# Gate table of the experts: one full fp32 product per token replaced by two rounded ones, and the work between them spread differently

## The chip, the cores and the metric

One NeuronCore of one Trainium2 chip runs the whole program in one launch. The metric is the device time in microseconds (us), median of three runs. Engines are named as the profile names them: PE (TensorE) with its weight loads PEld, DVE (VectorE), ACT (ScalarE), POOL (GpSimd) and SP (the queue that issues most DMAs).

## What is computed

Two transformer blocks on 512 tokens of width 1024. The part that the change touches is the expert layer of the first block: each token picks 128 experts (8 heads, 16 each) out of 16,384 = 128 x 128, with a gate value for each.

```python
    gate = jax.nn.softmax(top_s, axis=-1)
    def expert_block(args):
        xb, eb, gb = args
        act = jax.nn.gelu(jnp.einsum("pd,ped->pe", xb, jnp.take(u, eb, axis=0)), approximate=False)
        return jnp.einsum("pe,ped->pd", (gb * act).astype(v.dtype), jnp.take(v, eb, axis=0))
```

The kernel computes it densely: all 16,384 products u·x, a dense table of gates (zero where an expert was not picked), the product of both, and the dense product with v.

## The kernel before

The expert phase is the function `peer`. Activations lie transposed, features on the 128 partitions and the 512 tokens along a row. It has three parts.

**Front.** PE works through 16 query tiles and 128 "up" tiles of expert rows u. A tile is 24 matmuls (128x128 weights, 512 columns): a full fp32 product is made of three products of rounded fp32 (`F32R`), high x high, high x low, low x high (`parts_product`, L1125). The tile's way is fixed by semaphores: SP loads it into one of four ring slots, ACT writes its rounded high part (`high`, L1579), POOL subtracts to get the low part (L1451, 128x1024), PE multiplies, ACT applies Gelu from PSUM (L1593), SP stores the result to DRAM. High and low parts are double buffered: the parts of tile n+2 are made after PE has finished tile n. DVE meanwhile finds the top 16 of each head. `U_HEAD` = 6 up tiles per head are used there, `AHEAD` = 5 more before the gate table starts.

**Gate table.** The picked experts lie in `sel` (row number, column number, gate value, each 128 picks x 512 tokens after the transposes at L1539, copied from PSUM into `selt` by L1720). For each token the 128x128 gate table is a matrix product over its 128 picks: `rows` (0/1, 128 picks x 128) as the one operand, `cols` (the gate value where the column number fits, else zero) as the other. Eight tokens form a group, 64 groups in all. For a group DVE writes `rows` with one instruction (L1726, 128x1024, into half of the tile `h`) and `cols` with eight (L1730, 128x128 each, compare and multiply with two values per partition), PE makes eight plain fp32 matmuls of 128 columns (L1518, `gate`), ACT copies the group out of PSUM into `slab` (L1602). `rows`, `cols` and PSUM are double buffered: DVE may write group g once PE has finished g-2; PE may write group g once ACT has stored g-2. After every 16 groups (128 tokens, one of four stretches `tt`) ACT issues four DMAs of 2 MB that store the slab to DRAM (L1630), and waits for them before it stores the first group of the next stretch.

PE's program interleaves gate groups and up tiles by hand: `between(g)` says after which groups an up tile follows, `TAILS` how many follow after the sixteenth group of a stretch. Before, `between` is true for g % 8 in (0, 1, 3, 4, 6) and `TAILS` is (8, 8, 8, 11). The same two tables order ACT's Gelu and `high` work.

**Down.** 128 tiles of v, multiplied with gate table times activation; it begins after the last up tile.

Of the kernel before, what the change touches and what calls it, by code (L numbers as in the profile page):

```python
# [9 lines left out]
F32R = mybir.dt.float32r  # L10
ALU = mybir.AluOpType
# [3 lines left out]
P = 128  # L15
T = 512
# [1304 lines left out]
def peer(nc, K, d, ring):  # L1321
# [12 lines left out]
    with Phase(nc, "peer") as ph:  # L1334
# [1 line left out]
        wp = ph.sb("w_parts", [P, 2, 2, KT * P], F32R)  # L1336
        pp = ph.sb("act_parts", [P, 2, 2, T], F32R)
        slab = ph.sb("slab", [P, NKEY, P])
        sel = ph.sb("sel", [P, 3, TT, P])
        selt = ph.sb("selt", [P, 3, T])  # L1340
        cols = ph.sb("cols", [P, 2, G, NKEY])
        iota = ph.sb("iota", [P, NKEY])
        keys = ph.sb("keys", [P, 2, NKEY])
        stage = K.h[:, 0:4, :]
        rows = K.h[:, 4:8, :].rearrange("p (b x) t -> p b (x t)", b=2).rearrange("p b (g i) -> p b g i", g=G)

        flat = slab[:].rearrange("p i t -> p (i t)")
        at = [0]
# [51 lines left out]

        EARLY = PEER_H * U_HEAD
        AHEAD = 5
        TAILS = (8, 8, 8, 11)

        def between(g):

            return g % 8 in (0, 1, 3, 4, 6)

        assert EARLY + AHEAD + sum(TAILS) + TT * sum(between(g) for g in range(groups)) == U_TILES

# [64 lines left out]
        def _(pe):  # L1475
# [35 lines left out]
            def gate(g):  # L1511
                b = g % 2
                pe.wait_ge(rows_done, g + 1)
                pe.wait_ge(cols_done, g + 1)
                if g >= 2:
                    pe.wait_ge(g_stored, g - 1)
                for t in range(G):
                    last = nc.tensor.matmul(g_ps[:, b * 1024 + t * P:b * 1024 + (t + 1) * P], rows[:, b, t, :], cols[:, b, t, :],  # L1518
                                            start=True, stop=True)
                last.then_inc(g_done, 1)  # L1520

            n = 0
# [139 lines left out]
        def _(dve):  # L1662
# [55 lines left out]
            for w in range(3):  # L1718
                dve.wait_ge(tr_done, w + 1)
                V.tensor_copy(selt[:, w, :], t_ps[:, w * T:(w + 1) * T]).then_inc(tr_stored, 1)  # L1720
            dve.wait_ge(tr_stored, 3)
            for g in range(TT * groups):
                b = g % 2
                if g >= 2:
                    dve.wait_ge(g_done, g - 1)
                V.tensor_tensor(rows[:, b], iota[:].unsqueeze(1).to_broadcast([P, G, NKEY]),  # L1726
                                selt[:, 0, g * G:(g + 1) * G].unsqueeze(2).to_broadcast([P, G, NKEY]), ALU.is_equal).then_inc(rows_done, 1)
                for t in range(G):
                    one = slice(g * G + t, g * G + t + 1)
                    last = V.tensor_scalar(cols[:, b, t, :], iota[:], selt[:, 1, one], selt[:, 2, one], ALU.is_equal, ALU.mult)  # L1730
                last.then_inc(cols_done, 1)

            def weigh(n):
# [1140 lines left out]
```

## Time and profile before

| | |
|---|---|
| median of 3 runs | 4344.9 us (4344.23 to 4344.94) |
| profiled execution | 4345.56 us, its span 4344.0 us |
| PE busy / DVE / ACT / POOL, share of span | 88% / 53% / 38% / 23% |
| stretch of the gate table, 1531.6 to 2055.6 us | 524.0 us, PE busy 523.98 |
| DVE busy there | 295.3 us |
| POOL busy there | 179.0 us |

The granted clock of TensorE is 1.00 (2.4 GHz) through the whole stretch. A row of the groups reads: line, engine, operation, written tile <- read tiles, sizes, count | busy time in us, mean ns of one | idle time of the engine before it and what ended it. Plain fp32 matmuls at L1518 leave two records each, so 512 products show as x1024. Matmuls overlap in the pipeline: the pace is the distance between starts, not the mean duration.

### The profile page before, as it was taken

The page shows a single profiled execution, that of the slowest core. Times are in us where ns is not written, and L with a number is a line of the kernel's source. Part 1 is how long each engine was busy: PE and PEld are TensorE (multiplying, and loading weights), DVE is VectorE, ACT ScalarE, POOL GpSimd, SP SyncE. Part 2 cuts the span into 40 slices and gives each one's busy share as a digit, 9 for nine tenths or more (in the row PEclk, how much of TensorE's full clock was granted, in tenths as well). Part 3 has the DMA queues.
Part 4 walks back from the last instruction along what each step waited for, and adds up shares of the span by engine and source line. Part 5 has one row for each costly group of instructions (what it writes and reads, how often), then busy time and mean ns, then how long its engine had stood idle before and what let it go on. Part 6 is the DMA issues. An engine that isn't in the chain of part 4 may idle for free. (4 is left out here: it accounts for less than half of the span.)

```text
span 4344.0 us, 48140 instructions
## 1 busy us (share of the span) xinstructions
PE 3825.2 (88%) x17810; PEld 3089.1 (71%) x17810; DVE 2296.6 (53%) x3538; ACT 1670.5 (38%) x2292; POOL 1011.1 (23%) x560
## 2 busy tenths in 40 slices
PE   2999799789899999999999999777799963688998
PEld 1888677677688888887888888445577743566775
DVE  6555344445466576553777777423434346835242
ACT  6555454443322254443444444323322132333222
POOL 0222121153244433333444444100000014200000
PEclk9999899899999999999999999889899986899999
DMA  4111011144244434556888888300122221122221
GB/s 147 59 50 53 27 54 39 54 169 159 81 129 129 133 133 162 191 194 221 262 268 264 266 265 266 112 26 23 63 87 82 78 68 27 30 68 77 87 86 60
DMA packets 225918, 515.93 MB, mean 119 GB/s; under 512 B 23200, under 2 KB 98208, under 8 KB 223552
## 3 DMA queue, kind: packets, MB, share of 16 engines
q1 hardware_dynamic: 202336, 407.83, 29.5%
q0 software_dynamic: 18864, 68.69, 4.8%
q10 hardware_dynamic: 4528, 36.89, 2.1%
q8 instruction: 117, 1.92, 0.2%
q14 instruction: 73, 0.60, 0.0%
HBM read 439.15 MB, written 69.21 MB: 117 GB/s over the span
## 5 line engine op out<-in xcount | busy, mean ns | idle before, releaser
L1125 PE MATMUL peer_banks<-peer_h_parts,peer_w_parts 128*128 128x512 f32 x3456 | 800.3, 391 | 18.0 <-POOL peer_w_parts L1451 18.0
L1125 PEld LDWEIGHTS peer_banks<-peer_h_parts,peer_w_parts 128*128 128x128 f32 x3456 | 646.3, 188 | 151.4 <-POOL peer_w_parts L1451 18.8
L1125 PE MATMUL peer_banks<-peer_act_parts,peer_w_parts 128*128 128x512 f32 x3072 | 699.1, 390 | 9.4 <-DVE peer_act_parts L1745 9.4
L1125 PEld LDWEIGHTS peer_banks<-peer_act_parts,peer_w_parts 128*128 128x128 f32 x3072 | 578.3, 188 | 130.2 <-issue 9.8
L1451 POOL TENSOR_TENSOR peer_w_parts<-peer_raw,peer_w_parts 128x1024 fp32r<-128x1024 f32 x144 | 345.2, 2397 | 573.6 <-ACT peer_w_parts L1579 573.6
L1579 ACT ACTIVATE peer_w_parts<-peer_raw 128x1024 fp32r<-128x1024 f32 x272 | 286.9, 1055 | 390.7 <-PE peer_banks L1125 390.7
L1125 PE MATMUL mlp_ps<-h_parts,mlp_w_parts 128*128 128x512 f32 x1536 | 369.8, 404 | 46.5 <-DVE h_parts L1272 37.3
L1125 PE MATMUL mlp_ps<-hidden,mlp_w_parts 128*128 128x512 f32 x1536 | 365.0, 400 | 23.2 <-DVE mlp_w_parts L1253 23.2
L1125 PEld LDWEIGHTS mlp_ps<-h_parts,mlp_w_parts 128*128 128x128 f32 x1536 | 296.1, 193 | 121.0 <-DVE mlp_w_parts L1253 49.0
L1125 PEld LDWEIGHTS mlp_ps<-hidden,mlp_w_parts 128*128 128x128 f32 x1536 | 292.5, 191 | 95.7 <-issue 25.0
L175 POOL TENSOR_TENSOR peer_slab<-peer_slab 128x1024 f32<-128x1024 f32 x96 | 236.8, 2467 | 335.9 <-ACT peer_slab L182 335.6
L1740 DVE TENSOR_TENSOR peer_slab<-peer_slab 128x512 f32<-128x512 f32 x128 | 294.9, 2304 | 4.4 <-DMA peer_slab<-peer_gates 4.4
L1125 PE MATMUL hgrn_proj_ps<-h_parts,hgrn_w_parts 128*128 128x512 f32 x960 | 269.0, 412 | 21.1 <-POOL hgrn_w_parts L469 21.1
L1750 DVE TENSOR_TENSOR peer_w_parts<-peer_raw,peer_w_parts 128x1024 fp32r<-128x1024 f32 x128 | 156.9, 1226 | 241.2 <-ACT peer_w_parts L1579 241.2
L1593 ACT ACTIVATE h<-peer_banks 128x512 f32<-128x512 f32 x128 | 76.5, 598 | 489.3 <-PE peer_banks L1125 489.3
L1726 DVE TENSOR_TENSOR h<-peer_iota,peer_selt 128x1024 f32<-128x1024 f32 x64 | 166.9, 2608 | 166.5 <-PE peer_banks L1518 166.4
L1253 DVE TENSOR_TENSOR mlp_w_parts<-slots,mlp_w_parts 128x1024 fp32r<-128x1024 f32 x128 | 155.8, 1221 | 151.3 <-ACT mlp_w_parts L1224 151.3
L1224 ACT ACTIVATE mlp_w_parts<-slots 128x1024 fp32r<-128x1024 f32 x128 | 134.5, 1055 | 213.4 <-PE mlp_ps L1125 197.2
L1125 PEld LDWEIGHTS hgrn_proj_ps<-h_parts,hgrn_w_parts 128*128 128x128 f32 x960 | 167.8, 190 | 51.8 <-POOL hgrn_w_parts L469 21.5
L469 POOL TENSOR_TENSOR hgrn_w_parts<-x,hgrn_w_parts 128x1024 fp32r<-128x1024 f32 x40 | 102.4, 2562 | 371.7 <-ACT hgrn_w_parts L664 371.7
L1125 PE MATMUL gla_proj_ps<-h_parts,gla_w_parts 128*128 128x512 f32 (+1 forms) x600 | 171.1, 424 | 20.1 <-DVE gla_w_parts L942 14.9
L2398 POOL IOTA tables_steps<- 128x16 f32 x1 | 0.1, 144 | 719.6 <-POOLq L104 719.6
(518 smaller groups left out, 5735.5 us busy)
## 6 DMA issues: line engine op xcount, KB each, us to landing
peer_raw<-in_peer_u SPq DMA_DIRECT2D x128, 512.0 KB, 3.7
peer_raw<-in_peer_v SPq DMA_DIRECT2D x128, 512.0 KB, 5.3
slots<-in_mlp_w SPq DMA_DIRECT2D x128, 512.0 KB, 3.7
peer_slab<-in_w_mod POOLq DMA_DIRECT2D x96, 512.0 KB, 4.6
peer_acts<-h SPq DMA_DIRECT2D x128, 256.0 KB, 2.5
peer_gates<-peer_slab ACTq DMA_DIRECT2D x16, 2048.0 KB, 16.6
peer_slab<-peer_acts SPq DMA_DIRECT2D x128, 256.0 KB, 5.5
peer_slab<-peer_gates SPq DMA_DIRECT2D x128, 256.0 KB, 5.9
```

The costliest lines, as they stand in the source:

```text
L175: ins = V_.tensor_tensor(self.prod[:, u, :], self.ring[:, slot, :], self.rows[:, u, :], ALU.mult)
L469: nc.gpsimd.tensor_tensor(wp[:, m % 2, 1, :], ring[m % R], wp[:, m % 2, 0, :].bitcast(F32), ALU.subtract).then_inc(w_lo, 1)
L1125: last = nc.tensor.matmul(out, w(a, k), x(b, k), start=start and k == ks[0] and n == 0, stop=stop and k == ks[-1] and n == 2)
L1224: nc.scalar.activation(wp[:, s % 2, 0, :], raw[:, s % R, :], ACT.Copy).then_inc(w_hi, 1)
L1253: nc.vector.tensor_tensor(wp[:, s % 2, 1, :], raw[:, s % R, :], wp[:, s % 2, 0, :].bitcast(F32), ALU.subtract).then_inc(w_lo, 1)
L1451: nc.gpsimd.tensor_tensor(wp[:, p % 2, 1, :], ring.raw[:, p % R, :], wp[:, p % 2, 0, :].bitcast(F32), ALU.subtract).then_inc(w_lo, 1)
L1579: A(wp[:, p % 2, 0, :], ring.raw[:, p % R, :], ACT.Copy).then_inc(w_hi, 1)
L1593: A(stage[:, n % 4, :], a_ps[:, n % 2 * T:(n % 2 + 1) * T], ACT.Gelu).then_inc(gelu_done, 1)
L1726: V.tensor_tensor(rows[:, b], iota[:].unsqueeze(1).to_broadcast([P, G, NKEY]), selt[:, 0, g * G:(g + 1) * G].unsqueeze(2).to_broadcast([P, ...
L1740: V.tensor_tensor(wact[:, n % 2, :], act_in_sb[:, n % 4, :], gate_in_sb[:, n % 4].rearrange("p b t -> p (b t)"), ALU.mult).then_inc(weight ...
L1750: V.tensor_tensor(wp[:, p % 2, 1, :], ring.raw[:, p % R, :], wp[:, p % 2, 0, :].bitcast(F32), ALU.subtract).then_inc(v_lo, 1)
L2398: G.iota(steps[:], [[1, LB]], base=0, channel_multiplier=0, allow_small_or_imprecise_dtypes=True).then_inc(cst, 1)
```

## The change

Three edits, all in `peer`.

1. The gate value is split once for all tokens into a rounded high part and a low part (`selt` 3 and 4, one copy and one subtraction of 128x512 on DVE). `cols` is written twice for each token, once with each part, so DVE issues 16 instead of 8 instructions of 128x128 per group. `rows` and `cols` are now `F32R`.
2. PE multiplies the two with two rounded fp32 matmuls that accumulate into the same PSUM, in place of one plain fp32 matmul.
3. `between(g)` is true for seven of eight groups, and `TAILS` shrinks to (4, 4, 4, 7). The number of up tiles is the same.

Buffers move to make room: `sel` lies in `h`, `rows` has a tile of its own.

```diff
-        sel = ph.sb("sel", [P, 3, TT, P])
-        selt = ph.sb("selt", [P, 3, T])
-        cols = ph.sb("cols", [P, 2, G, NKEY])
+        selt = ph.sb("selt", [P, 5, T])
+        rows = ph.sb("rows", [P, 2, G, NKEY], F32R)
+        cols = ph.sb("cols", [P, 2, 2, G, NKEY], F32R)
...
-        rows = K.h[:, 4:8, :].rearrange("p (b x) t -> p b (x t)", b=2).rearrange("p b (g i) -> p b g i", g=G)
+        sel = K.h[:, 4:7, :].rearrange("p w (t n) -> p w t n", t=TT)
...
-        TAILS = (8, 8, 8, 11)
+        TAILS = (4, 4, 4, 7)
...
-            return g % 8 in (0, 1, 3, 4, 6)
+            return g % 8 != 7
...
-                    last = nc.tensor.matmul(g_ps[:, b * 1024 + t * P:b * 1024 + (t + 1) * P], rows[:, b, t, :], cols[:, b, t, :],
-                                            start=True, stop=True)
+                    for part in range(2):
+                        last = nc.tensor.matmul(g_ps[:, b * 1024 + t * P:b * 1024 + (t + 1) * P], rows[:, b, t, :], cols[:, b, part, t, :],
+                                                start=part == 0, stop=part == 1)
...
+            st.then(V.tensor_copy(selt[:, 3, :].bitcast(F32R), selt[:, 2, :]))
+            st.then(V.tensor_tensor(selt[:, 4, :], selt[:, 2, :], selt[:, 3, :], ALU.subtract))
...
-                    last = V.tensor_scalar(cols[:, b, t, :], iota[:], selt[:, 1, one], selt[:, 2, one], ALU.is_equal, ALU.mult)
+                    for part in range(2):
+                        last = V.tensor_scalar(cols[:, b, part, t, :], iota[:], selt[:, 1, one], selt[:, 3 + part, one], ALU.is_equal, ALU.mult)
```

On PE, the first stretch of the gate table before: L1518 is a gate group of 8 matmuls (x16 is two groups in a row), L1125 x24 an up tile, x192 the eight tiles of the tail.

```order
1120 L1518 MATMUL peer_banks<-peer_cols,h 128x128 x16
1121 L1125 MATMUL peer_banks<-peer_h_parts,peer_w_parts 128x512 x24
1122 L1518 MATMUL peer_banks<-peer_cols,h 128x128 x8
1123 L1125 MATMUL peer_banks<-peer_h_parts,peer_w_parts 128x512 x24
1124 L1518 MATMUL peer_banks<-peer_cols,h 128x128 x16
1125 L1125 MATMUL peer_banks<-peer_h_parts,peer_w_parts 128x512 x24
1126 L1518 MATMUL peer_banks<-peer_cols,h 128x128 x8
```

The same place after; L1519 is L1518 of before, a group is now 16 matmuls, so x32 is two groups in a row.

```order
1120 L1519 MATMUL peer_banks<-peer_cols,peer_rows 128x128 x16
1121 L1125 MATMUL peer_banks<-peer_h_parts,peer_w_parts 128x512 x24
1122 L1519 MATMUL peer_banks<-peer_cols,peer_rows 128x128 x16
1123 L1125 MATMUL peer_banks<-peer_h_parts,peer_w_parts 128x512 x24
1124 L1519 MATMUL peer_banks<-peer_cols,peer_rows 128x128 x32
1125 L1125 MATMUL peer_banks<-peer_h_parts,peer_w_parts 128x512 x24
1126 L1519 MATMUL peer_banks<-peer_cols,peer_rows 128x128 x16
```

Two groups stood together in three of eight places; now only the eighth and the ninth group of a stretch do.

On DVE, the start of the gate table before, from the copies of the transposed picks on:

```order
961 L1720 COPY peer_selt<-peer_banks 128x512 x3
962 L1726 TENSOR_TENSOR h<-peer_iota,peer_selt 128x1024
963 L1730 TENSOR_SCALAR peer_cols<-peer_iota,peer_selt 128x128 x8
964 L1726 TENSOR_TENSOR h<-peer_iota,peer_selt 128x1024
```

and after:

```order
961 L1721 COPY peer_selt<-peer_banks 128x512 x3
962 L1723 CAST peer_selt<-peer_selt 128x512
963 L1724 TENSOR_TENSOR peer_selt<-peer_selt 128x512
964 L1729 TENSOR_TENSOR peer_rows<-peer_iota,peer_selt 128x1024
```

Two instructions stand in front of the first group, and (in the rows that follow) sixteen L1734 where eight L1730 stood.

## Rows read from the trace of the kernel before

**Rows 1.** The page: busy time, clock in 40 slices.

```profile
PE 3825.2 (88%) x17810; PEld 3089.1 (71%) x17810; DVE 2296.6 (53%) x3538; ACT 1670.5 (38%) x2292; POOL 1011.1 (23%) x560
...
PEclk9999899899999999999999999889899986899999
```

**Rows 2.** Busy time by stretch, the four stretches of the gate table.

```profile
core 0: us, PE busy (x) PEld busy (x) DVE busy (x) ACT busy (x) POOL busy (x), PEclk, DMA share, GB/s
1531.60:1658.30 126.70, 126.68 (x687) 109.59 (x688) 77.90 (x153) 59.08 (x52) 43.03 (x18) 1.00 0.47 175
...
sum 524.00, PE 523.98 PEld 452.22 DVE 295.32 ACT 241.58 POOL 179.03; mean PE 130.99 PEld 113.05 DVE 73.83 ACT 60.40 POOL 44.76
```

**Rows 3.** Groups of instructions, 1531.6 to 2055.6 us.

```profile
L1125 PE MATMUL peer_banks<-peer_h_parts,peer_w_parts 128*128 128x512 f32 x1800 | 420.3, 392 | 0.0
...
L1451 POOL TENSOR_TENSOR peer_w_parts<-peer_raw,peer_w_parts 128x1024 fp32r<-128x1024 f32 x74 | 176.9, 2391 | 343.6 <-ACT peer_w_parts L1579 343.6
L1726 DVE TENSOR_TENSOR h<-peer_iota,peer_selt 128x1024 f32<-128x1024 f32 x63 | 164.4, 2610 | 166.4 <-PE peer_banks L1518 166.4
...
L1518 PE MATMUL peer_banks<-peer_cols,h 128*128 128x128 f32 x1024 | 121.4, 275 | 0.3 <-DVE peer_cols L1730 0.3
...
L1579 ACT ACTIVATE peer_w_parts<-peer_raw 128x1024 fp32r<-128x1024 f32 x75 | 78.8, 1050 | 0.0
L1593 ACT ACTIVATE h<-peer_banks 128x512 f32<-128x512 f32 x75 | 44.8, 598 | 273.0 <-PE peer_banks L1125 273.0
```

**Rows 4.** Timeline of PE: start us, us, engine, line, operation, count, idle before.

```profile
1531.62 2.02 PE L1518 MATMUL peer_banks<-peer_cols,h 128*128 128x128 f32 x16 [0.28 <-DVE peer_cols L1730]
...
1596.93 1.95 PE L1518 MATMUL peer_banks<-peer_cols,h 128*128 128x128 f32 x16
...
1604.19 3.73 PE L1518 MATMUL peer_banks<-peer_cols,h 128*128 128x128 f32 x32
...
1614.94 43.80 PE L1125 MATMUL peer_banks<-peer_h_parts,peer_w_parts 128*128 128x512 f32 x192
```

**Rows 5.** Rounded matmuls of 256 columns (timeline of PE), and two loads in a row (PEld).

```profile
154.09 3.04 PE L1125 MATMUL hgrn_proj_ps<-hc_parts,hgrn_w_parts 128*128 128x256 f32 x24
...
764.19 0.30 PEld L1125 LDWEIGHTS gla_proj_ps<-h_parts,gla_w_parts 128*128 128x128 f32 x2 [2.82 <-POOL gla_w_parts L469]
```

**Rows 6.** Timeline of DVE at the start of the gate table and in a free stretch.

```profile
1525.03 1.89 DVE L1720 COPY peer_selt<-peer_banks 128x512 f32<-128x512 f32 x3 [0.75 <-PE peer_banks L1539]
...
1532.54 4.23 DVE L1730 TENSOR_SCALAR peer_cols<-peer_iota,peer_selt 128x128 f32<-128x128 f32 x8
...
1540.95 3.32 DVE L1726 TENSOR_TENSOR h<-peer_iota,peer_selt 128x1024 f32<-128x1024 f32 x1 [0.99 <-PE peer_banks L1518]
...
1609.39 2.13 DVE L1730 TENSOR_SCALAR peer_cols<-peer_iota,peer_selt 128x128 f32<-128x128 f32 x8
1611.44 1.21 DVE L1726 TENSOR_TENSOR h<-peer_iota,peer_selt 128x1024 f32<-128x1024 f32 x1
1612.58 2.13 DVE L1730 TENSOR_SCALAR peer_cols<-peer_iota,peer_selt 128x128 f32<-128x128 f32 x8
```

**Rows 7.** Timeline of POOL over the same start.

```profile
1525.94 2.41 POOL L1451 TENSOR_TENSOR peer_w_parts<-peer_raw,peer_w_parts 128x1024 fp32r<-128x1024 f32 x1 [3.03 <-ACT peer_w_parts L1579]
1533.00 2.41 POOL L1451 TENSOR_TENSOR peer_w_parts<-peer_raw,peer_w_parts 128x1024 fp32r<-128x1024 f32 x1 [4.65 <-ACT peer_w_parts L1579]
1540.79 2.40 POOL L1451 TENSOR_TENSOR peer_w_parts<-peer_raw,peer_w_parts 128x1024 fp32r<-128x1024 f32 x1 [5.38 <-ACT peer_w_parts L1579]
```

**Rows 8.** DVE groups with rounded output, 512 elements.

```profile
L1837 DVE CAST hidden<-mlp_buf 128x512 fp32r<-128x512 f32 x16 | 6.8, 427 | 0.5
L1745 DVE TENSOR_TENSOR peer_act_parts<-peer_slab,peer_act_parts 128x512 fp32r<-128x512 f32 x128 | 87.6, 684 | 0.1
```

**Rows 9.** The slab's stores: timeline of ACT, and time to landing of all 16.

```profile
1615.22 2.05 ACT L1602 ACTIVATE peer_slab<-peer_banks 128x1024 f32<-128x1024 f32 x1 [0.24 <-PE peer_banks L1518]
1617.31 3.19 ACTq L1630 DMA_DIRECT2D peer_gates<-peer_slab  x4
...
DMA to landing us min/median/max: 7.6/16.6/24.8
```

**Rows 10.** Granted clock after idle times of PE: by stretch, then PE's timeline.

```profile
764.20:768.00 3.80, 3.80 (x20) 3.09 (x21) 1.28 (x2) 2.08 (x4) 1.70 (x1) 1.00 0.50 138
691.80:695.20 3.40, 3.40 (x10) 2.67 (x11) 1.23 (x1) 2.02 (x3) 1.31 (x1) 0.55 0.46 154
...
764.19 1.66 PE L1125 MATMUL gla_proj_ps<-h_parts,gla_w_parts 128*128 128x512 f32 x6 [2.40 <-POOL gla_w_parts L469]
691.80 2.93 PE L1125 MATMUL gla_proj_ps<-h_parts,gla_w_parts 128*128 128x512 f32 x6 [2.40 <-POOL gla_w_parts L469]
```

## The prediction

> **What bounds the kernel now.** I read the page first: PE is busy 88% of the span at nearly full clock [rows 1], so an edit on PE's work counts and one on another engine counts only where PE waits for it. Then the busy time by stretch over the gate table: in the 524 us from 1531.6 to 2055.6, PE is busy 523.98, at clock 1.00, DVE 295 and POOL 179 [rows 2]; the second and third stretch repeat the first within 0.1. Then the groups: PE waited 0.3 us for `cols` in the whole stretch, while DVE waited 166 us for PE [rows 3]. So PE alone sets this stretch, and DVE has slack. The questions are what a rounded matmul of 128 columns costs on PE, and whether DVE still has slack after the change.
>
> **PE's paces.** A group's 16 records last 1.95 us, the last of them 0.275 [rows 3, 4]: (1.95 - 0.275)/15 = 0.112 us from start to start, 1.79 a group. The eight up tiles of a tail are 192 matmuls in 43.80 us [rows 4], the last 0.39 [rows 3]: 0.227 each, 5.45 a tile. Check: group and tile together run from 1596.93 to 1604.19 [rows 4], 7.26, against 1.79 + 5.45 = 7.24.
>
> **Part 1, the matmuls.** Before there are 1024 records of 128 columns at L1518, after there are 1024 rounded ones (64 groups of 16). The trace has no rounded matmul of 128 columns. Two bounds from rows: its moving side may take a quarter of a 512-column one, 0.227/4 plus a few ns, 0.066 us; or it may cost what a full fp32 product costs, two records, 0.224. Between them: 24 rounded ones of 256 columns take 3.04 us, the last 0.29, so 0.120 each, and two weight loads in a row start 0.30 - 0.19 = 0.11 apart although PE had been idle before them [rows 5]. A new load of 128x128 thus seems not to follow another in less than 0.107 to 0.112 us, and each of these matmuls needs its own load. I take 0.112: nearest in kind are the load pair and today's records, which have the same load. PE's gate work then stays at 1.79 a group, and part 1 gives nothing.
>
> The Trainium skill (TensorE: Matmul & The Clock Gate, "Back-to-back issue gap") gives about 81 ns for a sustained stream of load and matmul at 128 columns. By it a group would be 1.30 us, and DVE's pace (below) would leave +10 us instead of the sum below. The load pair in this trace speaks for the slower figure.
>
> **Part 2, DVE.** A group costs DVE 1611.44 to 1612.58, 1.14 us, for `rows`, and 1609.39 to 1611.44, 2.05, for eight `cols` [rows 6], 0.256 each. After: 1.14 + 16 x 0.256 = 5.24. That the output is rounded should not matter: a rounding copy of 512 elements takes 427 ns where a two-input operation takes 684 [rows 8], so it keeps its double pace.
>
> DVE does not run alone. While POOL's 2.40 us subtraction runs [rows 7], a DVE instruction on SBUF stands still: `rows` of 1540.95 lasts 3.32 instead of 1.21, beside POOL's 1540.79; and the eight `cols` of 1532.54 last 4.23 instead of 2.13, beside POOL's 1533.00 [rows 6, 7]. Each POOL operation thus costs DVE 2.10 us, and POOL itself is not held up (mean 2.39 [rows 3]). There is one POOL operation per up tile. So DVE needs 5.24 + 2.10 = 7.34 us for a group with an up tile, PE 7.24. The slack is gone.
>
> **Part 3, the order.** With `between` at seven of eight, PE has 7 tiles and 7 groups from the end of the first group of an eight to the start of the next eight's first: 7 x 5.45 + 7 x 1.79 = 50.7 us. The eighth and ninth group stand together, and there DVE's debt is called in.
>
> - *Start.* DVE's copies end at 1526.95, and POOL runs until 1528.35 [rows 6, 7]. The new copy therefore ends near 1528.7, the subtraction (0.69) at 1529.5, `rows` at 1530.6. Sixteen `cols` take 4.1, and POOL's 1533.00 falls among them, +2.1: 1536.8, and PE starts the first group at 1536.9 instead of 1531.62. **+5.3.**
> - *Ninth group, first stretch.* DVE must make groups 1 to 8: 8 x 5.24 = 41.9, with seven POOL operations 14.7, less the 1.9 that it began ahead of the first group's end: 54.8 against 50.7. **+4.1.**
> - *Ninth group, three later stretches.* The tail's four tiles (21.8 us) let DVE fill both buffers, but no more, since it may run only two groups ahead. It then makes 7 groups, 36.7, with eight POOL operations (one from the last tile of the tail), 16.8: 53.5 against 50.7. **3 x 2.8 = +8.4.**
> - *Second eight.* DVE begins group 9 about 1.8 ahead; groups 9 to 15 take 36.7 + 6 x 2.1 = 49.3 less 1.8 = 47.5, and PE gets to the sixteenth after 7 x 5.45 + 6 x 1.79 = 48.9. No wait: **0**; less than 1.4 us of cover.
> - *The slab's store.* ACT issues it from 1617.31, 2.1 us after the group is done, and the last part lands up to 24.8 us after its own issue, which is near 1619.0 [rows 9]: 28.6 us after the group. Before, eight tiles (43.6) hid it. Now PE is through the next first group after 21.8 + 1.8 = 23.6, and ACT waits 5 us there, with Gelu and the next high part queued behind it. ACT's store (2.05), Gelu (0.6), high part (1.05) and POOL (2.4) [rows 3, 9] then end 34.7 after the group; PE asks for that tile at 23.6 + 5.45 + 1.79 + 5.45 = 36.3. Hidden by 1.6 us: **0**; if stores land 4 us later, 2.4 us three times.
> - *Clock.* PE now has one wait of 5.3 and four of 3 to 4 us. After a wait of 2.40 the clock once stayed at 1.00 and once fell to 0.55, which made six matmuls last 2.93 instead of 1.66 [rows 10]. At half that chance and about 1.3 to 1.7 us each, part of it hidden in DVE's lateness: **+2**, bounds 0 and 8.
> - *The rest.* Moved buffers, the last tail of seven tiles (38 us, before the down tiles need the slab) and the down part: 0, hidden by those seven tiles.
>
> **Sum.** 5.3 + 4.1 + 8.4 + 2 = 19.8, say 20 us. The profiled execution's span of 4344.0 becomes 4364, and with the 1.56 us around it 4365.6; it ran 0.7 above the median of 4344.9, so the median becomes 4365.
>
> Bounds of this case: if one POOL operation fewer falls into each eight, each of the four waits at the ninth group shrinks by 2.1, and without clock losses it is +9.4, 4354; one more in each and all the clock losses give 17.8 + 8.4 + 8 = 34, 4379. At 0.120 a record, PE's own work grows 64 x 0.13 = 8 us and the waits shrink by as much: the same total.
>
> **Rivals.**
> - *The load does not bind.* Records at 0.066 make a group 1.06 us. That would be 64 x 0.73 = 47 us less work for PE, but DVE still sets the pace: groups 2 to 15 of a stretch need 14 x 7.34 = 102.8, plus some 0.3 of hand-over, 1.06 for the last group, 21.8 of tail and 1.06 for the next first group = 127.0, against 126.7 before [rows 2]. With the start of 5.3 and 2 in the first stretch: +8, 4353. For it: moving 128 columns needs a quarter of 0.227. Against it: the two loads 0.11 apart. By the 81 ns of the Trainium skill's page named above this case would give +10, 4355.
> - *Faster (the other side).* As above, and DVE keeps up. It decides at DVE's group of 5.45 + 1.06 = 6.5 us: with 5.24 of its own, a POOL operation may then hold it only 1.27 instead of 2.10. Then -47 + 5.3 = -42, 4303. Against it: both POOL overlaps read above cost 2.10.
> - *Slow rounded matmuls.* Below some width a rounded matmul costs a full fp32 product, 0.224: groups of 3.58, 64 x 1.79 = 115 more, the waits at the ninth group vanish, the start stays: +120, 4465. Against it: 256 columns still run at 0.120; nothing shows 128.
> - *`cols` at single pace.* If rounded output costs the double pace, each gets (684 - 427)/4 = 64 ns longer: a group of 6.27, 8.37 with POOL, so 14 x 8.37 = 117.2 per stretch where 102.8 stood, four times +14.4, on top of about 17: +75, 4420. Against it: the rounding copy's 427 ns [rows 8].
>
> **Chances.** Forecast (0.107 to 0.12 a record, DVE a little too slow) 0.70; load does not bind 0.12; faster 0.04; slow matmuls 0.09; `cols` at single pace 0.05. A difference of 0.2% (8.7 us) is about what a measurement of this kernel can tell from none; 4353.6 is that bound. Same: the 0.12 and 0.02 of the forecast's low end; slower: 0.68 + 0.09 + 0.05. The range reaches from 4350, which takes in the case of the free load, to 4382; it leaves out 0.18, the two slow cases and the faster one.
>
> **What the changed kernel's profile would show.** The distance between the 16 records of a group (0.112; 0.066 or 0.224 by the rivals) and the counts of the group, x1024. `cols` x1024 at a pace of 0.256. DVE busy in the gate stretch at about 64 x 5.24 + 2.1 per up tile, some 485 us, and nearly no idle time in the first eights. PE idle before the gate matmuls 17 to 20 us, released by `cols`, in five places: one of 5 and four of 3 to 4. ACT waiting about 5 us for the slab's stores three times, and nobody behind it. The forecast is wrong if PE's idle time sits before every group (DVE slower than 7.34), if it is zero (POOL holds DVE less), or if PE's busy time in the stretch changes by more than 10 us.

## The result, and the profile after

The changed kernel took 4382.66 us (median of 4 runs, 4382.01 to 4383.82) where the kernel before took 4344.92 in the same rounds (4344.23 to 4349.78): a ratio of 1.0085, 95% interval 1.0067 to 1.0102. That is slower by 37.7 us. The forecast was slower by 20, 4365; the direction held, and 18 us were missing in its sum. The measured time is also 0.7 us above the upper end of the stated range, 4382. The profiled execution took 4382.01 us, its span 4380.4, so the two spans are 36.4 apart.

The page of after. PE has 16 us more of busy time and DVE 174; POOL and ACT are within 5 us of where they were [rows 1].

```profile
PE 3841.4 (88%) x17810; PEld 3099.9 (71%) x17810; DVE 2470.6 (56%) x4052; ACT 1673.2 (38%) x2292; POOL 1015.7 (23%) x560
...
PEclk8999899899999999999999999889899986899999
```

The groups of instructions from 1531.6 to 2095.0 us, to be read beside [rows 3] (line, engine, operation, names, sizes, count | busy us, mean ns | idle time before, and what ended it):

```profile
L1125 PE MATMUL peer_banks<-peer_h_parts,peer_w_parts 128*128 128x512 f32 x1800 | 432.6, 398 | 0.0
L1734 DVE TENSOR_SCALAR peer_cols<-peer_iota,peer_selt 128x128 fp32r<-128x128 f32 x1017 | 383.1, 451 | 0.0
...
L1519 PE MATMUL peer_banks<-peer_cols,peer_rows 128*128 128x128 f32 x1024 | 130.2, 283 | 18.4 <-issue 12.8 <-DVE peer_cols L1734 5.6
...
L1729 DVE TENSOR_TENSOR peer_rows<-peer_iota,peer_selt 128x1024 fp32r<-128x1024 f32 x63 | 93.6, 1486 | 50.5 <-PE peer_banks L1519 50.5
```

Two things changed places. PE waited 0.3 us ahead of the gate matmuls and now waits 18.4; DVE waited 166 us for PE and now waits 50. The profile puts only the first of PE's waits down to DVE and 12.8 us to "issue", which means that it shows no releaser. DVE's timeline names one all the same: at the second stretch's ninth group its last `cols` ends at 1729.24 (1722.94 + 6.30, the row stands with e9 below), 0.1 us ahead of PE's start. And PE's busy time grew although its work did not: the up tiles' 1800 matmuls are 432.6 us instead of 420.3, the 1024 gate records 130.2 instead of 121.4. The timeline of PE shows why. Its rows around the first group of the table, and around the ninth group of the first two stretches:

```profile
1535.99 3.65 PE L1519 MATMUL peer_banks<-peer_cols,peer_rows 128*128 128x128 f32 x16 [5.63 <-DVE peer_cols L1734]
1539.44 7.69 PE L1125 MATMUL peer_banks<-peer_h_parts,peer_w_parts 128*128 128x512 f32 x24
1546.97 1.90 PE L1519 MATMUL peer_banks<-peer_cols,peer_rows 128*128 128x128 f32 x16
1548.70 5.71 PE L1125 MATMUL peer_banks<-peer_h_parts,peer_w_parts 128*128 128x512 f32 x24
...
1595.67 3.65 PE L1519 MATMUL peer_banks<-peer_cols,peer_rows 128*128 128x128 f32 x16 [3.09 <-issue]
1599.12 6.93 PE L1125 MATMUL peer_banks<-peer_h_parts,peer_w_parts 128*128 128x512 f32 x24
...
1729.34 3.65 PE L1519 MATMUL peer_banks<-peer_cols,peer_rows 128*128 128x128 f32 x16 [3.23 <-issue]
1732.78 6.66 PE L1125 MATMUL peer_banks<-peer_h_parts,peer_w_parts 128*128 128x512 f32 x24
...
1862.74 3.65 PE L1519 MATMUL peer_banks<-peer_cols,peer_rows 128*128 128x128 f32 x16 [3.23 <-issue]
1866.18 8.13 PE L1125 MATMUL peer_banks<-peer_h_parts,peer_w_parts 128*128 128x512 f32 x24
```

An undisturbed group is 1.90 us and an undisturbed tile 5.71 (1546.97 and 1548.70). Behind each wait the group takes 3.65 and the tile 6.66 to 8.13. The busy time by stretch says what that is: granted clock 0.50, the lower of the two levels (1.2 GHz), behind each wait (columns as in [rows 2], the clock third from the end):

```profile
1536.00:1540.00 4.00, 4.00 (x18) 3.90 (x19) 4.00 (x14) 0.32 (x1) 0.00 (x0) 0.50 0.29 113
1595.70:1600.00 4.30, 4.30 (x18) 4.19 (x19) 4.30 (x15) 0.64 (x1) 0.00 (x0) 0.50 0.39 126
1729.30:1733.00 3.70, 3.66 (x17) 3.69 (x18) 3.70 (x12) 0.00 (x0) 0.00 (x0) 0.50 0.51 142
```

**Where 37.5 us went.** The down part starts at 2102.57; before, it started at 2065.08 (behind that point the profiled execution makes up 1.1 us, which I have not traced). Between the start of the gate table and there:

| | us |
|---|---|
| the tile ahead of the first group starts earlier | -1.0 |
| wait for the first group, 5.63 instead of 0.28 | +5.35 |
| waits for the four ninth groups, 3.09 + 3 x 3.23 | +12.8 |
| clock: group and tile behind each of the five waits, over 1.90 + 5.71: 3.7, 3.0, 2.7, 4.2, 3.3 | +16.9 |
| wait of the down part, 10.58 instead of 9.40 | +1.2 |
| PE's own pace: the new order (+0.5 in e2 below), and a rounded group, start to start of its tile, 1.74 instead of 1.70; what is left over | +2.2 |
| sum | +37.5 |

The fifth wait stands at 1997.61, with 3.62 and 7.33 behind it. The wait of the down part, before and then after:

```profile
2065.08 11.13 PE L1125 MATMUL peer_banks<-peer_act_parts,peer_w_parts 128*128 128x512 f32 x37 [9.40 <-DVE peer_act_parts L1745]
```

```profile
2102.57 7.73 PE L1125 MATMUL peer_banks<-peer_act_parts,peer_w_parts 128*128 128x512 f32 x24 [10.58 <-DVE peer_act_parts L1749]
```

The gate stretch itself reads 1535.99 to 2053.60, PE busy 504.84 of 517.61, DVE busy 463. With the last tail, up to 2091.99, PE is busy 543.2 us for the same 2824 matmul records that took 524.1 before: 19 us more, nearly all of it the clock's term in the table.

### The profile page after: what moved, and what is told of

Same layout as the page of the kernel before. It is cut to its first block and busy times, and to the rows that moved or that the text cites. A ratio compares the mean times of both kernels' runs of the same rounds, so it can differ in the third digit from the quotient of the medians.

```text
span 4380.4 us, 48654 instructions
## 1 busy us (share of the span) xinstructions
PE 3841.4 (88%) x17810; PEld 3099.9 (71%) x17810; DVE 2470.6 (56%) x4052; ACT 1673.2 (38%) x2292; POOL 1015.7 (23%) x560
## 5 line engine op out<-in xcount | busy, mean ns | idle before, releaser
L1125 PE MATMUL peer_banks<-peer_h_parts,peer_w_parts 128*128 128x512 f32 x3456 | 812.5, 395 | 17.9 <-POOL peer_w_parts L1451 17.9
L1125 PEld LDWEIGHTS peer_banks<-peer_h_parts,peer_w_parts 128*128 128x128 f32 x3456 | 651.3, 190 | 154.4 <-POOL peer_w_parts L1451 18.8
L1125 PE MATMUL peer_banks<-peer_act_parts,peer_w_parts 128*128 128x512 f32 x3072 | 698.6, 390 | 10.6 <-DVE peer_act_parts L1749 10.6
L1125 PEld LDWEIGHTS peer_banks<-peer_act_parts,peer_w_parts 128*128 128x128 f32 x3072 | 578.0, 188 | 131.2 <-issue 11.0
L1125 PE MATMUL mlp_ps<-h_parts,mlp_w_parts 128*128 128x512 f32 x1536 | 369.8, 404 | 46.5 <-DVE h_parts L1272 37.3
L1125 PE MATMUL mlp_ps<-hidden,mlp_w_parts 128*128 128x512 f32 x1536 | 364.9, 400 | 23.3 <-DVE mlp_w_parts L1253 23.3
L1734 DVE TENSOR_SCALAR peer_cols<-peer_iota,peer_selt 128x128 fp32r<-128x128 f32 x1024 | 384.9, 450 | 0.0
L1125 PEld LDWEIGHTS mlp_ps<-h_parts,mlp_w_parts 128*128 128x128 f32 x1536 | 296.2, 193 | 120.9 <-DVE mlp_w_parts L1253 49.0
L1125 PEld LDWEIGHTS mlp_ps<-hidden,mlp_w_parts 128*128 128x128 f32 x1536 | 292.4, 191 | 95.8 <-issue 25.0
L1125 PE MATMUL hgrn_proj_ps<-h_parts,hgrn_w_parts 128*128 128x512 f32 x960 | 268.8, 412 | 20.1 <-POOL hgrn_w_parts L469 20.1
L1125 PEld LDWEIGHTS hgrn_proj_ps<-h_parts,hgrn_w_parts 128*128 128x128 f32 x960 | 167.7, 190 | 50.8 <-POOL hgrn_w_parts L469 20.5
L1125 PE MATMUL gla_proj_ps<-h_parts,gla_w_parts 128*128 128x512 f32 (+1 forms) x600 | 175.5, 432 | 20.0 <-DVE gla_w_parts L942 14.8
```

The costliest lines, as they stand in the source:

```text
L1125: last = nc.tensor.matmul(out, w(a, k), x(b, k), start=start and k == ks[0] and n == 0, stop=stop and k == ks[-1] and n == 2)
L1734: last = V.tensor_scalar(cols[:, b, part, t, :], iota[:], selt[:, 1, one], selt[:, 3 + part, one], ALU.is_equal, ALU.mult)
```

## The experiments

My theory after the result had three parts: (a) DVE makes the waits: its sixteen `cols` plus POOL's hold are a little more than PE's group and tile; (b) each wait costs its own length and then some 3 us again, since the clock falls behind it; (c) rounding, spread and buffers by themselves cost nothing. The rivals: the rounded matmuls are slower in some way that the waits hide; the other order of tiles collides with something (the slab's stores, the down part); the waits alone cost, and the longer tiles have another cause. All ratios are against the kernel before in the same rounds.

### e1: the same matmuls, half the DVE work

```diff
-                    for part in range(2):
-                        last = V.tensor_scalar(cols[:, b, part, t, :], iota[:], selt[:, 1, one], selt[:, 3 + part, one], ALU.is_equal, ALU.mult)
+                    last = V.tensor_scalar(cols[:, b, 0, t, :], iota[:], selt[:, 1, one], selt[:, 3, one], ALU.is_equal, ALU.mult)
...
-                        last = nc.tensor.matmul(g_ps[...], rows[:, b, t, :], cols[:, b, part, t, :], start=part == 0, stop=part == 1)
+                        last = nc.tensor.matmul(g_ps[...], rows[:, b, t, :], cols[:, b, 0, t, :], start=part == 0, stop=part == 1)
```

> The changed kernel, but DVE writes only the high part of cols (8 instead of 16 instructions a group) and PE multiplies with it twice: PE's instructions stay, half of DVE's work on cols goes. It leaves out the low parts of the gate values and counts the high parts twice. Theory (DVE's pace of 5.24 + 2.10 us a group makes PE wait, and each wait brings the clock down): DVE needs 3.19 + 2.10 = 5.3 against PE's 7.28, so no wait of over 1 us and no fall of the clock in the gate stretch: 4344 us, within 3. Rival 1 (rounded matmuls of 128 columns are dearer on PE than their pace shows): still near 4382. Rival 2 (the new order of groups and tiles costs by itself): still above 4360.

Measured: 4351.28 us, ratio 1.0014 (1.0005 to 1.0024), 6 above before and 4 above the upper end that I expected. Nearly all of the 37.7 is gone with eight of 16 DVE instructions, while PE runs the same 1024 rounded matmuls in the same order. The waits at the ninth groups are zero and PE is busy 484.20 of 484.20 us at full clock from 1536.2 to the last group. What stays is the start: PE's timeline shows one wait of 1.48 us for the first group, and even behind that one the clock fell, though not at once: it reads 0.93 from 1531.14 to 1533.00, while the group runs, and 0.50 from 1533 to 1536, in the tile.

```profile
1531.14 2.18 PE L1519 MATMUL peer_banks<-peer_cols,peer_rows 128*128 128x128 f32 x16 [1.48 <-DVE peer_cols L1733]
1533.12 7.11 PE L1125 MATMUL peer_banks<-peer_h_parts,peer_w_parts 128*128 128x512 f32 x24
...
1536.20:2020.40 484.20, 484.20 (x2633) 417.38 (x2632) 325.10 (x559) 229.31 (x198) 160.84 (x67) 1.00 0.45 162
```

The 5 us by which its down part starts later than before's are this wait (+1.2), its clock (2.18 + 7.11 for 1.90 + 5.71, +1.7), PE's own pace (+2.2, as in the table) and the wait of the down part (11.13, +1.7), less 1.7 by which the front was done sooner. So (a) holds, and the rounded matmuls are not the cause: e1's stretch without its wait and its clock is 526.1 us, e2's with plain fp32 and the same order (below) 524.6, so the rounding is worth 1.5 us.

### e2 and e3: the order of the tiles by itself, and its absence

e2 is the kernel before with only the new order, as below; e3 is the kernel after with the same two lines turned back.

```diff
-        TAILS = (8, 8, 8, 11)
+        TAILS = (4, 4, 4, 7)
...
-            return g % 8 in (0, 1, 3, 4, 6)
+            return g % 8 != 7
```

> The kernel before with the new order alone: a tile after seven of eight groups, tails of 4, 4, 4, 7. Theory: sixteen more changes between group and tile at 0.11 us each, nothing else: +1.8, 4347 us, and ACT waits some 5 us for the slab's stores three times without anyone behind it. Rival 2 (the order costs): 4360 or more, with PE idle after the tails.

> The changed kernel with the old order: a tile after five of eight groups, tails of 8, 8, 8, 11. Theory: two groups in a row come three times in eight, and DVE needs over 5.2 us for each where PE needs 1.73; in each eight DVE takes 8 x 5.24 + 5 x 2.1 = 52.4 where PE takes 8 x 1.73 + 5 x 5.56 = 41.6, and the two filled buffers help once per stretch: +74 of waits, plus clock losses that DVE's lateness partly hides: 4420 to 4440 us. Rival 2 (the new order is what costs): 4350 or less.

e2 measured 4345.75, ratio 1.0001 (0.9991 to 1.0010); e3 measured 4446.66, ratio 1.0230 (1.0213 to 1.0247). The order costs nothing that the medians tell (its stretch in the trace is 524.6 us against 524.1) and gives nothing without the DVE work; with it, it saves 64 us. In e2 ACT waits for the slab's stores, as in after, and nobody waits for ACT. In e3, PE's timeline shows waits ahead of second groups of pairs that stand without a tile between, 58 us in sum with the first group's 5.63: four of 5.3 to 5.4, twelve near 2.5 and four of 0.3, and the clock's mean over the stretch is 0.91:

```profile
1614.20 3.65 PE L1519 MATMUL peer_banks<-peer_cols,peer_rows 128*128 128x128 f32 x16 [5.38 <-issue]
...
1536.75:2100.00 563.25, 510.88 (x2560) 438.67 (x2560) 427.80 (x1071) 223.22 (x191) 150.97 (x63) 0.91 0.37 134
```

It came out 7 us above the upper end that I expected, on the side where each wait costs its clock too. Each of the seventeen waits of 2.4 us and more was followed by the lower clock. Behind the shorter ones it often came only some 2 us after PE had started again: behind the wait of 2.46 that ended at 1788.41 the clock reads 0.98 for two microseconds and 0.50 for the next two.

### e4: plain fp32 matmuls beside the sixteen DVE instructions

The kernel before with the new order, in the buffers of after, plain fp32; DVE writes each `cols` twice, PE uses one of them.

```diff
-                    last = V.tensor_scalar(cols[:, b, t, :], iota[:], selt[:, 1, one], selt[:, 2, one], ALU.is_equal, ALU.mult)
+                    for part in range(2):
+                        last = V.tensor_scalar(cols[:, b, part, t, :], iota[:], selt[:, 1, one], selt[:, 2, one], ALU.is_equal, ALU.mult)
```

> The kernel before (plain fp32 matmuls, one per token) with the new order, and DVE writes cols twice, the second time into a buffer that nobody reads: 16 instructions a group. Theory: as long as the changed kernel, since only DVE's pace matters: waits of about 4.5 and 4 x 3, five falls of the clock: 4380 us, within 5. Rival 1 (the rounded matmuls cost): as the new order alone, 4347.

Measured: 4374.31, ratio 1.0067 (1.0050 to 1.0083). No rounded operand is in it, and it has the same picture: a first wait of 4.48 (it lacks the two instructions that split the gate value, 1.2 us), then four of 3.43, and a fallen clock behind all five (behind the first stretch's ninth group it came within the group, which took 2.53, and its tile 6.94).

```profile
1725.54 3.76 PE L1518 MATMUL peer_banks<-peer_cols,peer_rows 128*128 128x128 f32 x16 [3.43 <-issue]
1728.95 6.86 PE L1125 MATMUL peer_banks<-peer_h_parts,peer_w_parts 128*128 128x512 f32 x24
```

It lies 8 us under after, 0.7 below the lower end of what I expected, and 29 above before. Together e1 and e4 say it from both sides: the rounding without the DVE work costs 6 us at most, the DVE work without the rounding 29.

### e5 and e6: what a gate matmul costs

e5 has e1's DVE work and splits each token's product into two matmuls of 64 columns, so the count of loads stays and half of the columns goes. e6 has the same DVE work and one rounded matmul for each token: half of the loads.

```diff
+                    for c in range(2):
+                        at = b * 1024 + t * P + c * 64
+                        last = nc.tensor.matmul(g_ps[:, at:at + 64], rows[:, b, t, :], cols[:, b, 0, t, c * 64:(c + 1) * 64],
+                                                start=True, stop=True)
```

```diff
+                    last = nc.tensor.matmul(g_ps[:, b * 1024 + t * P:b * 1024 + (t + 1) * P], rows[:, b, t, :], cols[:, b, 0, t, :],
+                                            start=True, stop=True)
```

> As the run with half of the cols work (high parts only, low parts left out), but each token's product is made of two rounded matmuls of 64 columns each over the same rows, so 16 matmuls a group again, each with a weight load of 128x128. It shows what sets the pace of 0.11 us. Theory (the load sets it): the pace stays at 0.107 to 0.112 although the columns are halved, the group stays at 1.74 us, 4351 us as the run with half of the cols work, within 3. Rival (the columns set it): half of 0.11, 0.055 to 0.066 a record, a group of about 1 us, 64 x 0.75 = 48 us less: 4303.

> As the run with half of the cols work, but PE multiplies once per token: 8 rounded matmuls a group. It leaves out the low parts of the gate values. Theory (PE alone sets the stretch as soon as DVE is in time, 0.11 a record): 512 records less at 0.11, 56 us less than 4351: 4295, within 4; DVE needs 5.3 a group against PE's 6.4. Rival (something else than PE is next, the slab's store or DVE): over 4305, with PE idle time in front of tiles or groups.

e5: 4352.37, ratio 1.0016 (1.0007 to 1.0026). e6: 4293.07, ratio 0.9878 (0.9861 to 0.9894). PE's timeline has a group of 16 matmuls of 64 columns (e5), then of 8 of 128 columns (e6):

```profile
1625.74 1.87 PE L1520 MATMUL peer_banks<-peer_cols,peer_rows 128*128 128x64 f32 x16
```

```profile
1623.68 1.00 PE L1518 MATMUL peer_banks<-peer_cols,peer_rows 128*128 128x128 f32 x8
```

Half the columns save 0.03 us of 1.90 a group; half the matmuls save 0.90. So each rounded matmul costs 0.11 us with its load, whatever its columns. That it is the load, and not some other fixed cost, the kernel before shows in its first layers and its state tables. Loads and matmuls of other sizes, the loads first:

```profile
138.75 0.19 PEld L507 LDWEIGHTS hgrn_score_ps<-hgrn_e_x 128*64 128x64 f32 x2
```

```profile
3631.74 8.46 PE L2342 MATMUL tables_k_ps<-tables_cd,tables_bd 128*32 128x128 f32 x76
```

Two loads of 64 columns start 0.055 apart (0.19 less the 0.134 that one of them lasts), half of the 0.11 of 128 columns, so a load's time goes with its columns. The second row warns against reading too much into the plain fp32 product of before: these are plain fp32 matmuls of 128 columns with loads of only 32, and still 0.109 apart. A plain fp32 record of 128 columns thus needs its 0.11 for its columns alone. Two rounded matmuls cost what one plain product cost because 0.11 for the load happens to meet 0.11 for the columns; by these rows only the rounded one would gain from a cheaper load, which no run here tries.

The Trainium skill (TensorE: Matmul & The Clock Gate, "LDWEIGHTS (loading the stationary operand)") gives a load as P / 1.2 in ns, P being its columns, so 107 ns for 128; e5's 0.11 and the 0.055 for 64 columns bear it out. The 81 ns that the Trainium skill (same page, "Back-to-back issue gap") gives for a stream at 128 columns, weighed in the prediction, is not reached by any rounded or plain fp32 group here. e6 is 52 us faster than the kernel before: each group takes 0.85 instead of 1.70 us from its start to its tile, 64 times 0.85 = 54. That is the price of one of the two products, and what the change could have brought on PE had one been enough.

### e7: the waits filled with idle matmuls

After, with matmuls of no use issued ahead of PE's waits, 24 ahead of the first group and 12 ahead of each ninth.

```diff
+                for _ in range(24 if g == 0 else 12 if g % 16 == 8 else 0):
+                    nc.tensor.matmul(banks[:, 6 * T:7 * T], hp[:, 0, 0, 0:P], hp[:, 0, 0, :], start=True, stop=True)
                 pe.wait_ge(rows_done, g + 1)
```

> The changed kernel, with matmuls that nobody reads in the places where PE waits: 24 rounded ones of 512 columns (5.45 us) in front of the first group, 12 (2.7 us) in front of the ninth group of each stretch, into an unused bank of PSUM. The waits for cols stay, only PE is not idle in them. Theory (the waits cost 18 us and the falls of the clock behind them another 17): 17 us less than the changed kernel's 4382.7: 4366, within 3, clock 1.00 through the stretch. Rival (the lower clock is hidden by DVE's lateness): 4380 or more.

Measured: 4368.36, ratio 1.0052 (1.0035 to 1.0069): more work on PE, and 14.3 us faster than after. DVE's part is as it was, so the difference is the clock. PE's timeline at the second stretch's ninth group shows the wait filled, 0.33 us left, and group and tile at full pace behind it:

```profile
1721.57 2.99 PE L1514 MATMUL peer_banks<-peer_h_parts 128*128 128x512 f32 x12
1724.88 1.97 PE L1521 MATMUL peer_banks<-peer_cols,peer_rows 128*128 128x128 f32 x16 [0.33 <-issue]
1726.69 5.70 PE L1125 MATMUL peer_banks<-peer_h_parts,peer_w_parts 128*128 128x512 f32 x24
```

The one place where the filler was too short, the first stretch's ninth group, left 1.33 us, and there the clock fell:

```profile
1592.58 2.10 PE L1521 MATMUL peer_banks<-peer_cols,peer_rows 128*128 128x128 f32 x16 [1.33 <-issue]
1594.47 7.19 PE L1125 MATMUL peer_banks<-peer_h_parts,peer_w_parts 128*128 128x512 f32 x24
```

The table's 16.9 us for the clock less this 1.7 (2.10 + 7.19 over 1.90 + 5.71) would be 15.2; 14.3 were won, and the rest is about what the fall at the start hides (see below). That settles (b).

### e8 and e9: DVE's pace against PE's

e8 puts a tile behind every group, so that no two groups stand together. e9 halves POOL's subtraction in the gate table's tiles (the second half of their low parts is left out); by its trace the two operations at 1532.25 and 1549.00, beside the first groups, are still whole, and the first half one starts at 1556.29.

```diff
-        TAILS = (4, 4, 4, 7)
+        TAILS = (3, 3, 2, 3)
...
-            return g % 8 != 7
+            return True
```

```diff
+                w = KT * P // 2 if p >= QU + 8 else KT * P
-                nc.gpsimd.tensor_tensor(wp[:, p % 2, 1, :], ring.raw[:, p % R, :], wp[:, p % 2, 0, :].bitcast(F32),
+                nc.gpsimd.tensor_tensor(wp[:, p % 2, 1, 0:w], ring.raw[:, p % R, 0:w], wp[:, p % 2, 0, 0:w].bitcast(F32),
```

> The changed kernel with a tile after every group (eight of eight) and tails of 3, 3, 2, 3. Theory: without two groups in a row PE's 7.29 a group nearly meets DVE's 7.34, so the four waits at the ninth group and their falls of the clock go; the wait at the start (5.6) and its 3.7 of clock stay, the slab's store costs about 2.5 in the stretch with three tiles behind it: 4358 to 4362 us. Rival (DVE is behind everywhere, the place of the wait is chance): waits spread over the groups, still near 4380.

> The changed kernel, but from just before the gate table on POOL subtracts only the first half of each up tile's low part (128x512 instead of 128x1024); the second half of the low parts is left out (what stood there before is used). DVE's and PE's instructions stay. Theory (POOL's operation holds DVE for nearly its own length): held 0.9 instead of 2.1 us a group, DVE needs 6.1 against PE's 7.28, so the four waits at the ninth group and their falls of the clock go; at the start the wait shrinks from 5.6 to 4.4: 4357 us, within 4. Rival (DVE's own 16 instructions are the bound, POOL's share is small): over 4370, waits at the ninth groups.

e8: 4363.36, ratio 1.0041 (1.0027 to 1.0055). The four waits at the ninth groups are gone, since PE reaches them 5.45 us later, and with them their clock. It came out 1 us above what I expected. Around the tail of only two tiles the slab's stores do reach PE: ACT spends 5.1 us on issuing them and then waits 9.7 us for them, and behind each of the two PE stands for POOL's low part, 0.43 and 0.90 us, without a fall of the clock. The last stretch pays with a tail of three tiles, and the down part's wait grows:

```profile
1950.31 5.74 PE L1125 MATMUL peer_banks<-peer_h_parts,peer_w_parts 128*128 128x512 f32 x24 [0.90 <-POOL peer_w_parts L1451]
...
2081.47 2.04 PE L1125 MATMUL peer_banks<-peer_act_parts,peer_w_parts 128*128 128x512 f32 x4 [14.38 <-DVE peer_act_parts L1749]
```

e9: 4354.54, ratio 1.0024 (1.0014 to 1.0033). DVE's timeline, sixteen `cols` a row. Of after, first those of the second stretch's ninth group, beside a whole POOL operation, then a row of the first stretch with none beside it; then a row of e9, beside half an operation:

```profile
1722.94 6.30 DVE L1734 TENSOR_SCALAR peer_cols<-peer_iota,peer_selt 128x128 fp32r<-128x128 f32 x16
...
1596.63 4.18 DVE L1734 TENSOR_SCALAR peer_cols<-peer_iota,peer_selt 128x128 fp32r<-128x128 f32 x16
```

```profile
1606.54 5.23 DVE L1735 TENSOR_SCALAR peer_cols<-peer_iota,peer_selt 128x128 fp32r<-128x128 f32 x16
```

With no POOL operation beside them they take 4.18 (the second row), with a whole one 2.1 more, with a half one (1.33 us) 1.05 more. Half the hold makes DVE's group 6.3 us against PE's 7.3, and all four waits at the ninth groups vanish; only the start stayed, 5.62, where POOL's operation is still whole. e9 shows that the 2.1 us that POOL holds DVE decide whether the waits exist.

### e10: a tile of slack ahead of the table

One more up tile ahead of the first group, one fewer in the last tail (the loops that issue the tiles follow; not shown).

```diff
-    AHEAD = 5
+    AHEAD = 6
-        TAILS = (4, 4, 4, 7)
+        TAILS = (4, 4, 4, 6)
```

> The changed kernel with two up tiles instead of one between the transposes and the first group, taken from the last tail (4, 4, 4, 6). Theory: the second tile's 5.45 us covers the wait of 5.6 at the start and the clock does not fall there (3.7); the four waits at the ninth group stay: 9 less than 4382.7, 4373 us, within 3. Rival (the start's wait is not lost but only moved, since DVE's lateness catches up at the ninth group): 4380.

Measured: 4379.13, ratio 1.0075 (1.0058 to 1.0092), between its theory and its rival, nearer to the rival. The start wait is gone, with its clock. But the ninth group's wait in the first stretch became 5.45 instead of 3.09:

```profile
1536.85 1.98 PE L1519 MATMUL peer_banks<-peer_cols,peer_rows 128*128 128x128 f32 x16 [0.24 <-DVE peer_cols L1736]
...
1544.31 1.97 PE L1519 MATMUL peer_banks<-peer_cols,peer_rows 128*128 128x128 f32 x16
...
1596.24 3.64 PE L1519 MATMUL peer_banks<-peer_cols,peer_rows 128*128 128x128 f32 x16 [5.45 <-issue]
```

From 1536.85 to 1544.31 group and tile take 7.46 us, where PE's own work is 7.26 [rows 4] and 0.035 more for the rounded group. DVE's timeline there has `rows` and `cols` of one group, 1.13 and 6.3 to the next start:

```profile
1544.09 1.21 DVE L1731 TENSOR_TENSOR peer_rows<-peer_iota,peer_selt 128x1024 fp32r<-128x1024 f32 x1
1545.22 6.41 DVE L1736 TENSOR_SCALAR peer_cols<-peer_iota,peer_selt 128x128 fp32r<-128x128 f32 x16
```

PE goes at DVE's pace in this stretch, with no wait that the rows show. The tile gave PE something to do while DVE was late, and DVE, whose work did not shrink, was late again at the next place where two groups stand together. The last tail's tile was taken from the down part, whose wait rose to 12.57. So of the 9 us of the start, 3.5 came out.

## Why the prediction was right in sign and short by 18 us

The result stands at the very edge: 4382.66 against a range that ended at 4382, and above the 4379 to which the prediction's own worst case for this mechanism added up. The 3 us between 4379 and 4382 come from no term. What was right is the mechanism of the waits; one term, the clock, was too small by 15 us. One of the prediction's own signs of being wrong came true with it: PE's busy time in the stretch changed by 19 us, and more than 10 was named as such a sign.

**PE's pace: right.** It took 0.112 us a record from the pair of loads; measured are 0.110 to 0.114 in all stretches (only the first two of a group are 0.057 apart), and e5 with the loads of 64 columns shows that the load binds. The rivals "the load does not bind" and "slow rounded matmuls" both fall with it.

**DVE's pace: right.** Forecast were 5.24 a group and 2.10 for each POOL operation; measured are 1.14 + 4.1 and 2.1 to 2.2 (6.30 instead of 4.18 above). The rivals "`cols` at single pace" and "faster" fall: the first for 4.18, the second for the 2.1. e9 is the proof from the other side: at 1.05 us of hold the waits at the ninth groups are gone. (DVE's busy time, 463 us, is 22 less than the 485 forecast; I have not taken that apart.)

**The places of the waits: right; their lengths in sum.** Forecast were 5.3 at the start, 4.1 and three of 2.8 at the ninth groups, none in the second eights. Measured are 5.35, 3.09 and three of 3.23. The sum, 18.1 where 17.8 stood, is partly luck: the first ninth group's wait is 1.0 shorter than forecast and the three others 0.4 longer each, for which I have no reason. The first is shorter because the clock fell at the start: DVE had both buffers full and waited 2.57 us for the slower PE, and then had the rest of the 3.7 us that PE lost to the clock as a gain. DVE's timeline of after:

```profile
1548.90 3.37 DVE L1729 TENSOR_TENSOR peer_rows<-peer_iota,peer_selt 128x1024 fp32r<-128x1024 f32 x1 [2.57 <-PE peer_banks L1519]
```

In e7, where nothing fell at the start, PE is through its eighth group at 1588.25 and starts the ninth at 1592.58: 4.3, the 4.1 of the prediction. And 4.3 - 3.7 + 2.57 is 3.2, near the 3.09 of after.

**The slab's stores: right.** ACT waited as forecast, at the first group of the three later stretches, 5.4 for the 5 of the prediction, and nobody stood behind it. ACT's timeline at the second stretch:

```profile
1680.36 2.00 ACT L1603 ACTIVATE peer_slab<-peer_banks 128x1024 f32<-128x1024 f32 x1 [5.40 <-DMA peer_gates<-peer_slab]
```

e2 has the same wait (5.43) and costs nothing. How narrow that was, e8 shows: behind a tail of two tiles instead of four, the stores reach PE.

**The clock: the term that was mis-sized.** The sum had +2 with bounds 0 and 8; measured are 16.9, twice the upper bound, and e7 wins 14.3 of them back by filling the waits. Two things went wrong in that step. I took [rows 10] as a coin toss, one fall in two waits, while here all five waits were followed by one. And I priced a fall at 1.3 to 1.7 us from a row of six matmuls, when the fallen clock reached over a whole group and most of a tile: 1.75 us on the group and 1.0 to 2.4 on the tile, 2.7 to 4.2 in all. I also thought that part of it would be hidden in DVE's lateness. At the start 1.1 us was, as worked out above. Behind a ninth group nothing can be, since PE waits for DVE nowhere in the second eight.

**Set at zero, and not zero.** The down part's wait grew by 1.2 us with the last tail four tiles shorter. The runs put an order on it: tails of 11, 7, 6 and 3 tiles end in 9.4, 10.6 to 11.1, 12.6 and 14.4 us of wait (before; after, e1 and e2; e10; e8). The moment at which DVE is free is not what counts: in after it finishes its last group some 50 us earlier, and then waits for the gate table to come back from DRAM, as its timeline shows:

```profile
2099.55 0.69 DVE L1744 TENSOR_TENSOR peer_slab<-peer_slab 128x512 f32<-128x512 f32 x1 [4.71 <-DMA peer_slab<-peer_gates]
```

And PE's own pace is 2.2 us longer, 0.5 by the order and most of the rest by the rounded groups. Neither is near the size of the clock's term.

**What stays open.** What decides whether the clock stays full behind a short wait: the first stretch of [rows 10] had such a case at 2.40 us, while all twelve waits near 2.5 in e3, the 1.48 of e1 and the 1.33 of e7 brought a fall. Waits under one microsecond (0.24 in e10, 0.33 and 0.46 in e7, 0.43 and 0.90 in e8) never did.

## What to carry to other kernels

- Price a wait on PE at its length plus what the clock costs behind it. Here waits of 3 us cost 6, and the cheapest way to see the second half is to fill the wait with matmuls of no use.
- When an edit brings a hidden engine close to the pace of the one that bounds, add up its group with everything that holds it, and go to the place where the bound engine has least between two demands. Here the two were within 0.1 us of each other at the tiles, so DVE built up no lead there, and at each pair of groups, where PE asks again after 1.74 us and DVE needs at least 5.2, it cost 6 us. A tile moved to hide one such place only sent the debt to the next; e8, which took away the pairs, and e9, which made DVE faster, worked.
- For small rounded matmuls count the loads: at 128 columns and at 64 each matmul costs its load's 0.11 us. A plain fp32 product of 128 columns is two records of 0.11 by its columns alone, so splitting it into two rounded matmuls wins nothing at this width.

## What I had not expected of the hardware

- The clock fell to half behind a wait of 1.48 us (e1) and one of 1.33 us (e7), some 2 us after PE had started again, and a fall after 3 us cost 2.7 to 4.2 us.
- A rounded matmul of 64 columns was as dear as one of 128 columns: 16 in 1.87 us against 1.90.
- PE can run at DVE's pace, 7.46 us for group and tile instead of 7.29, with no idle time in the rows between.
